# An opening with fifteen early rows of modulation and later bias flips, and the two heads of an attention unit issued apart

## The chip, the core and the metric

The kernel runs on one core of a Trainium2 chip. The metric is the device time of one execution in microseconds (us); a core has a TensorE (PE), a VectorE (DVE), a ScalarE (ACT), a GpSimd (POOL), a SyncE (SP) that here only issues DMAs, and 16 DMA engines. Each engine works through its own list of instructions in order; between engines there are only semaphores.

## The reference

One sequence of 256 tokens, 1024 features, float32, goes through two layers of one model and one of another. What matters here is the start of the first layer:

```python
shift, scale, gate = split(silu(c) @ ada_w[0, 0] + ada_b[0, 0], 3)      # c: 1024, ada_w: 1024 x 3072
h = rms_norm(x, norm_w[0, 0]) * (1 + scale) + shift
x = x + gate * hybrid_attention_mixer(h, ...)      # h @ w_in, gated linear attention, and
                                                   # sliding-window attention, 8 heads on 2 kv heads,
                                                   # scores + rel_bias[t5_bucket(distance)], then @ w_out
```

The mixer's product `h @ w_in` has 2,320 columns. The bias of the windowed attention depends only on the distance of query and key: a table of 32 buckets by 8 heads is spread over distances. Two MLPs, a pooling mixer, a second attention (8 heads, its own bias of position), retention and a gated feed-forward part follow.

## The kernel before

**Weight blocks.** Every large product runs over weight blocks of 1024 x 256 (1 MB). SP loads block n into `raw[n % 4]`; ACT copies it into a rounded high part (`split_hi`, L1897), DVE subtracts to get the low part (`split_lo`, L1215), and PE makes three products per tile: high by high, high by low, low by high (`product`, L595 to L597; with tokens as rows, L677 to L679). A block is 48 products of 256 columns. Activations are split too: `h_hi` by ACT, `h_lo` by DVE. PE needs `lo_done` of a block before it starts it.

**Banks.** PE writes the blocks to the four G banks of PSUM and all small results to four A banks. Each A bank has a fixed order of uses, written out with `take`: PE waits with `bank_empty` until the use before was read, readers wait with `bank_full` and release with `bank_read`.

**Modulation.** `silu(c) @ ada_w` is made on DVE: `ada_w` comes as 24 rows of blocks, 128 x 1024 each (512 KB), and `ada_sum` multiplies one by a value of `c_silu` for each partition and adds it to an accumulator (L1234; the first of a part is L1229). Rows 0 to 7 are the scale, 8 to 15 the shift, 16 to 23 the gate. POOL issues the loads (L522) into three buffers `ada_raw` in turn, each after the row before in that buffer was used; eight rows, named in `ADA_EARLY`, have places of their own in `raw[1]` to `raw[3]`, `GE` and `GG` and are asked for at once (L530). `ada_next(count)` in DVE's list sets when the sums are made. The sum over partitions is left: `turn_sums` has PE transpose the accumulator (L705, 8 transposes) into two A banks, and `part` on DVE reduces each bank along its row (L1260) and adds the bias. ACT has another form of that reduction, `rows_along` (L1912), used in later layers only.

**The opening.** SP issues constants, `c`, x, thirteen small loads of vectors, `rel_bias`, the gate's small weights, then (after DVE has copied the table out of its bank) the table's write to DRAM, weight block 0, and, after ten modulation rows are used, the read of the shifted bias rows, 1 MB, each partition one element further (`hankel`, which is `MIX`). PE transposes x (L781), the vectors, makes the table, the mean squares (L803), the scale's transposes, four `flip` products of 512 columns that turn the bias rows over (L810), the shift's transposes, eight clock-keeping products (`keep_clock`, L622), and block 0 with a wait before each pair of feature tiles. The normalised pairs are made by DVE (x times gain times root, L1377), rounded by ACT with the shift added (`high_norm`, L1934) and subtracted by DVE (L1360). ACT copies the flips to `BIAS` (L2006) before it. Behind block 0 come the gate's rank product, a transpose, block 1 and the logits.

**Attention.** A unit is a pair of heads and a block of 128 queries: `scores` (L737), bias, maximum, exponent and scale on DVE and ACT, `turned` (transposes, L749) and `weighted` (L759). The two heads of a unit lie in the two halves of the partitions and write one bank. Inside `scores`, PE waits for the first head's product before it issues the second's:

```python
for e in range(2):
    ...
    last = pe.matmul(dst[:, e, 0:keys], Q4[half, hp, b * P:b * P + P], K4[half, kt, 0:keys], start=True, stop=True)
    if e == 0:
        chain(last)
```

In the first layer the eight units are written out by hand between the halves of blocks 2 to 8 (`first_half`, `second_half`); in the later attention, `attention(1, v)` on PE puts scores of unit v, transposes of v - 1 and the output of v - 2 behind one another between blocks. The gate's transposes stand between the halves of blocks 2 and 3.

## Time and profile before

| what | us |
|---|---|
| median of 3 runs (947.22 to 949.34) | 948.78 |
| the profiled execution | 948.3 |
| its span, first to last instruction | 946.6 |
| PE busy, share | 893.9, 94% |
| DVE / ACT / POOL busy | 684.8 / 463.6 / 84.5 |
| mean granted TensorE clock, of full | 0.991 |

Times in rows are us from the start of the span, of one execution. "Idle before" says what ended the wait of an engine in front of an instruction. Durations of matmuls overlap; the distance between starts is what counts.

### The profile page before, as it was taken

How to read it: one execution, taken by the hardware profiler on the slowest of the kernel's cores; microseconds unless marked ns; L12 is line 12 of the kernel's file. 1: busy time of each engine (PE TensorE's matmuls, PEld its weight loads, DVE VectorE, ACT ScalarE, POOL GpSimd, SP SyncE). 2: the span in 40 equal slices, each digit the busy share in tenths (PEclk: the TensorE clock that was granted, in tenths of full speed). 3: DMA queues.
4: the chain of work that ended last, by engine and by line, in shares of the span. 5: the costliest groups of instructions: out<-in, count | busy, mean ns of one | idle time of the engine just before them, and what ended most of it. 6: DMA issues, size and time to landing. Idle time of an engine off the chain costs nothing.

```text
span 946.6 us, 17770 instructions
## 1 busy us (share of the span) xinstructions
PE 893.9 (94%) x7084; PEld 855.4 (90%) x7084; DVE 684.8 (72%) x857; ACT 463.6 (49%) x623; POOL 84.5 (9%) x140
## 2 busy tenths in 40 slices
PE   2699989899999999899999999999999999999996
PEld 2488879899999999799999999888989999999996
DVE  4889888788897887766665556765587777775665
ACT  2348464466663335466653334544565444444445
POOL 2210148211110110000000000000000000000000
PEclk9899999999999999999999999999999999999998
DMA  9895754499996886277655553844435655655531
GB/s 340 301 358 185 243 200 158 139 318 320 327 359 232 311 305 218 74 238 222 222 200 178 181 188 119 254 135 134 134 109 166 201 188 182 199 166 177 162 119 44
DMA packets 156603, 196.64 MB, mean 208 GB/s; under 512 B 5341, under 2 KB 143116, under 8 KB 156556
## 3 DMA queue, kind: packets, MB, share of 16 engines
q1 hardware_dynamic: 142732, 145.64, 48.1%
q0 software_dynamic: 13824, 50.34, 14.2%
q8 instruction: 33, 0.54, 0.2%
q14 instruction: 14, 0.11, 0.0%
HBM read 194.90 MB, written 1.06 MB: 207 GB/s over the span
## 4 chain that ended last, share of the span: by engine, by line
PE 77%; DVE 10%; ACT 5%; DMA 4%; issue 3%; SPq 1%; POOL 0%; ACTq 0%; DVEq 0%; POOLq 0%
PE G L595 14%; PE G L597 14%; PE G L596 14%; PE A L595 7%; PE A L597 7%; PE A L596 7%; DVE w_lo L1215 3%; ACT w_hi L1897 2%; PE G L677 2%; PE G L678 2%; PE G L679 2%; PE A L737 2%; DMA ada_raw<-in_ada_w_dram 1%; DMA sinks<-in_attn_sinks_dram 1%; DVE ada_acc L1234 1%
## 5 line engine op out<-in xcount | busy, mean ns | idle before, releaser
L1215 DVE TENSOR_TENSOR w_lo<-raw,w_hi 128x2048 fp32r<-128x2048 f32 x135 | 307.0, 2274 | 159.3 <-ACT w_hi L1897 158.8
L1897 ACT ACTIVATE w_hi<-raw 128x2048 fp32r<-128x2048 f32 x135 | 256.5, 1900 | 246.5 <-PE G L597 130.0
L595 PE MATMUL G<-h_hi,w_hi 128*128 128x256 f32 x864 | 248.8, 288 | 9.3 <-DVE h_lo L1360 6.8
L596 PE MATMUL G<-h_lo,w_hi 128*128 128x256 f32 x864 | 245.1, 284 | 0.0
L597 PE MATMUL G<-h_hi,w_lo 128*128 128x256 f32 x864 | 245.0, 284 | 0.0
L595 PEld LDWEIGHTS G<-h_hi,w_hi 128*128 128x128 f32 x864 | 166.2, 192 | 15.6 <-DVE h_lo L1360 6.5
L596 PEld LDWEIGHTS G<-h_lo,w_hi 128*128 128x128 f32 x864 | 166.4, 193 | 0.2 <-issue 0.2
L597 PEld LDWEIGHTS G<-h_hi,w_lo 128*128 128x128 f32 x864 | 166.3, 193 | 0.0
L595 PE MATMUL A<-u_hi,w_hi 128*128 128x256 f32 x512 | 145.3, 284 | 1.6 <-DVE X L1338 1.2
L596 PE MATMUL A<-u_lo,w_hi 128*128 128x256 f32 x512 | 144.1, 282 | 0.0
L597 PE MATMUL A<-u_hi,w_lo 128*128 128x256 f32 x512 | 144.1, 281 | 0.0
L595 PE MATMUL G<-e_hi,w_hi 128*128 128x256 f32 x368 | 104.1, 283 | 0.0
L596 PE MATMUL G<-e_lo,w_hi 128*128 128x256 f32 x368 | 104.1, 283 | 0.0
L597 PE MATMUL G<-e_hi,w_lo 128*128 128x256 f32 x368 | 104.1, 283 | 0.0
L595 PEld LDWEIGHTS A<-u_hi,w_hi 128*128 128x128 f32 x512 | 96.4, 188 | 3.5 <-DVE X L1338 1.8
L596 PEld LDWEIGHTS A<-u_lo,w_hi 128*128 128x128 f32 x512 | 96.4, 188 | 0.0
L597 PEld LDWEIGHTS A<-u_hi,w_lo 128*128 128x128 f32 x512 | 96.4, 188 | 0.0
L1234 DVE SCALAR_TENSOR_TENSOR ada_acc<-ada_raw,c_silu,ada_acc 128x1024 f32<-128x1024 f32 x52 | 66.1, 1281 | 9.5 <-DMA ada_raw<-in_ada_w_dram 8.5
L595 PEld LDWEIGHTS G<-e_hi,w_hi 128*128 128x128 f32 x368 | 70.7, 192 | 0.0
L596 PEld LDWEIGHTS G<-e_lo,w_hi 128*128 128x128 f32 x368 | 70.7, 192 | 0.0
L597 PEld LDWEIGHTS G<-e_hi,w_lo 128*128 128x128 f32 x368 | 70.7, 192 | 0.0
L595 PE MATMUL A<-f_hi,w_hi 128*128 128x256 f32 x176 | 50.0, 284 | 1.6 <-DVE HN L1332 1.6
(349 smaller groups left out, 1389.7 us busy)
## 6 DMA issues: line engine op xcount, KB each, us to landing
raw<-in_mlp_w_dram SPq DMA_DIRECT2D x64, 1024.0 KB, 5.5
ada_raw<-in_ada_w_dram POOLq DMA_DIRECT2D x88, 512.0 KB, 5.3
raw<-in_w_in_dram SPq DMA_DIRECT2D x14, 1024.0 KB, 5.0
raw<-in_w_up_dram SPq DMA_DIRECT2D x11, 1024.0 KB, 5.3
raw<-in_w_gate_dram SPq DMA_DIRECT2D x11, 1024.0 KB, 5.4
raw<-in_attn_w_in_dram SPq DMA_DIRECT2D x9, 1024.0 KB, 10.3
raw<-in_w_down_dram SPq DMA_DIRECT2D x8, 1024.0 KB, 5.2
raw<-in_attn_w_out_dram SPq DMA_DIRECT2D x4, 1024.0 KB, 5.2
```

Of the source, the lines that this page charges most:

```text
L595: pe.matmul(dst, wh, ah, start=start, stop=False)
L596: pe.matmul(dst, wh, al, start=False, stop=False)
L597: return pe.matmul(dst, wl, ah, start=False, stop=stop)
L677: pe.matmul(dst, h_hi[:, t, toks], w_hi[n % 2][:, t, cols], start=t == 0, stop=False)
L678: pe.matmul(dst, h_hi[:, t, toks], w_lo[n % 2][:, t, cols], start=False, stop=False)
L679: last = pe.matmul(dst, h_lo[:, t, toks], w_hi[n % 2][:, t, cols], start=False, stop=t == KT - 1)
L737: last = pe.matmul(dst[:, e, 0:keys], Q4[half, hp, b * P:b * P + P], K4[half, kt, 0:keys], start=True, stop=True)
L1215: dve.tensor_tensor(w_lo[n % 2][:, 0:k, :], raw[n % RAW][:, 0:k, :], w_hi[n % 2][:, 0:k, :].bitcast(F32), ALU.subtract).then_inc(lo_done, 1)
L1234: dve.scalar_tensor_tensor(out=acc, in0=src, scalar=c_silu[:, bass.ds(i * 2 + k, 1)], in1=acc, op0=ALU.mult, op1=ALU.add).then_inc(ada_use ...
L1897: act.activation(w_hi[n % 2][:, 0:k, :], raw[n % RAW][:, 0:k, :], ACT.Copy).then_inc(hi_done, 1)
```

## The change

- Fifteen modulation rows (3 to 15, 19 and 20) have places of their own: five in `raw[1]` to `raw[3]`, the rest in buffers that attention uses later. POOL asks for all but row 15 at once; for that one it waits for the table's write, since it shares its place.
- SP's order becomes constants, c, `rel_bias`, small loads, the table's write, x, block 0, the gate's small loads, the bias rows; then it waits until row 14 has landed, and loads blocks 1 to 3 once the rows in their places are used.
- POOL makes x times root (four products of 128 x 512) in place of DVE, and waits for weight block 1 before it asks for row 16. ACT applies gain and shift in one operation and does it twice, for `h_hi` and for a float32 copy `HN1`, from which DVE subtracts in one operation a pair. The scale's sums and half of the shift's are reduced by ACT (`rows_along`).
- PE: the table first, x behind the vectors; eight clock-keeping products more behind the scale's transposes; the four flips behind block 0; ACT copies them behind the keys of block 0.
- The gate's transposes go behind the last unit of the first attention, ahead of block 9; ACT reduces them ahead of the split of block 10.
- `scores` takes a head. The wait goes from the first head's issue to the second's, which is placed in the next block behind two of its eight steps (six products), or behind other small products.

```diff
-ADA_EARLY = (3, 4, 5, 6, 7, 8, 19, 20)
+ADA_EARLY = (*range(3, 16), 19, 20)
...
-                 for n in range(6)] + [b[:, :, :].rearrange("p t s -> p (t s)") for b in (GE, GG)]
+                 for n in range(5)]
+        early += [b[:, :, :].rearrange("p t s -> p (t s)") for b in (Q4, K4, V4, GV)] + [
+            PT[:, :, :, :].rearrange("p a b s -> p (a b s)"),
+            wide[:, 4:6, :].rearrange("p a b -> p (a b)"), wide[:, 6:8, :].rearrange("p a b -> p (a b)"),
+            SS[:, :, :, :].rearrange("p a b s -> p (a b s)")]
+        early += [b[:, :, :].rearrange("p t s -> p (t s)") for b in (GE, GG)]
...
@@ SP
-                sp.dma_start(x_rows, x[0].rearrange("(k p) d -> p k d", p=P)).then_inc(x_in, 16)
+                sp.dma_start(rb[:, :], rel_bias).then_inc(rb_in, 16)
...
+                bank_was_read(sp, "table")
+                sp.dma_start(scratch.ap(), t8[:, :]).then_inc(table_out, 16)
+                sp.dma_start(x_rows, x[0].rearrange("(k p) d -> p k d", p=P)).then_inc(x_in, 16)
+                load(N_ATTN, w_in[:, :, ATTN_COLS[0]:ATTN_COLS[0] + COLS])
...
-                sp.wait_ge(ada_used, 10)
                 sp.dma_start(hankel[:, :, :],
...
+                sp.wait_ge(early_full[ADA_EARLY.index(2 * DT - 2)], 16)
...
-                        sp.wait_ge(ada_used, (14, 16, 16)[j - 1])
+                        sp.wait_ge(ada_used, (5, 7, 8)[j - 1])
@@ POOL
+                if f == 2 * DT - 1:
+                    pool.wait_ge(table_out, 16)
+                if f == 2 * DT:
+                    pool.wait_ge(rstd_ready, 1)
+                    for p in range(4):
+                        pool.tensor_tensor(HN0[:, 2 * p:2 * p + 2, :], X[:, 2 * p:2 * p + 2, :],
+                                           spread(rstd[:, :], 2), ALU.mult).then_inc(norm_ready, 1)
+                    pool.wait_ge(raw_full[1], 16)
@@ PE, a block's tile
                 for a, (kb, ka) in enumerate(kts):
+                    if inside and a == 2:
+                        scores(*inside)
@@ PE, scores(r, v, e)
+                if e == 0:
+                    bank_empty(pe, f"scores{r}{v}")
+                else:
+                    pe.wait_ge(score_first, ATT_UNITS * r + v + 1)
...
+                if e == 0:
+                    last.then_inc(score_first, 1)
+                else:
+                    bank_done(f"scores{r}{v}", last)
@@ PE, attention(r, v)
-                    scores(r, v)
+                    scores(r, v, 0)
                 if 1 <= v <= ATT_UNITS:
                     turned(r, v - 1)
+                if v < ATT_UNITS:
+                    scores(r, v, 1)
@@ PE, order
             turn_sums(0, "scale", DT)
-            pe.wait_ge(table_in, 16)
-            for q in range(4):
-                dst = bank_empty(pe, f"flip{q}")
...
-            turn_sums(0, "shift", 2 * DT)
+            keep_clock(0, 8)
+            turn_sums(0, "shift", 2 * DT)
             keep_clock(0, 8)
             feature_block(0, 0, split="n0")
+            pe.wait_ge(table_in, 16)
+            for q in range(4):
+                dst = bank_empty(pe, f"flip{q}")
...
-            scores(0, 0)
-            first_half(2)
-            scores(0, 1)
-            second_half(2)
-            turn_sums(0, "gate", ADA_B)
+            scores(0, 0, 0)
+            first_half(2, inside=(0, 0, 1))
+            scores(0, 1, 0)
+            second_half(2, inside=(0, 1, 1))
...
             weighted(0, 7)
+            turn_sums(0, "gate", ADA_B)
@@ DVE
-            chain(part(0, "scale"))
-            factor(0)
-            split_lo(0)
-            ada_next(4)
-            part(0, "shift").then_inc(mod_ready, 1)
...
+            ada_next(9)
+            for half in "ab":
+                bank_was_read(dve, f"scale0{half}")
+            chain(with_bias(DT, DT, DT))
+            chain(factor(0))
+            ssq[0] = 4
+            ada_next(2)
+            split_lo(0)
...
-            norm("n0", 0, GAIN[:, 0, :], MOD[:, 0, 0:DT])
+            for p in range(4):
+                low_pair("n0", p, HN1[:, 2 * p:2 * p + 2, :])
...
-            chain(part(0, "gate"))
@@ ACT
+            root(0)
+            for half in range(2):
+                src = bank_full(act, f"scale0{'ab'[half]}")
+                bank_read(f"scale0{'ab'[half]}", rows_along(src, DT + 4 * half))
...
+            src = bank_full(act, "shift0a")
+            bank_read("shift0a", rows_along(src, 0))
             act.wait_ge(mod_ready, 1)
-            high_norm("n0", MOD[:, 0, 0:DT])
+            for p in range(4):
...
+                for dst in (h_hi, HN1):
+                    for t in (2 * p, 2 * p + 1):
+                        ins = act.activation(dst[:, t, :], HN0[:, t, :], ACT.Identity,
+                                             scale=GAIN[:, 0, t:t + 1], bias=MOD[:, 0, t:t + 1])
+                ins.then_inc(hhi_ready, 1)
...
+            for half in range(2):
+                src = bank_full(act, f"gate0{'ab'[half]}")
+                bank_read(f"gate0{'ab'[half]}", rows_along(src, 2 * DT + 4 * half))
             split_hi(10)
```

`with_bias` adds the bias to sums that `rows_along` left; it exists before.

## Rows read from the trace of the kernel before

**Rows 1.** The page's first part: busy time of each engine over the span.
```profile
PE 893.9 (94%) x7084; PEld 855.4 (90%) x7084; DVE 684.8 (72%) x857; ACT 463.6 (49%) x623; POOL 84.5 (9%) x140
```

**Rows 2.** PE timeline to 55 us: start, us, line, op, tiles, count, [idle before].
```profile
12.13 1.97 PE L781 MATMUL A<-C,wide 128*128 128x128 f32 x8 [7.61 <-DMA wide<-in_x_dram]
...
35.97 5.32 PE L810 MATMUL A<-MIX,C 128*128 128x512 f32 x8 [7.47 <-DMA MIX<-bias_rows]
41.12 1.04 PE L705 MATMUL A<-C,ada_acc 128*128 128x128 f32 x8
41.99 3.62 PE L622 MATMUL G<-C,ones 128*128 128x256 f32 x16
...
50.88 0.38 PE L595 MATMUL G<-h_hi,w_hi 128*128 128x256 f32 x1 [0.15 <-DVE h_lo L1360]
...
54.57 0.28 PE L595 MATMUL A<-h_hi,g_hi 128*16 128x256 f32 x1
```

**Rows 3.** DVE timeline: the sixteenth modulation row, block 15.
```profile
39.59 1.28 DVE L1234 SCALAR_TENSOR_TENSOR ada_acc<-ada_raw,c_silu,ada_acc 128x1024 f32<-128x1024 f32 x1 [1.15 <-DMA ada_raw<-in_ada_w_dram]
```

**Rows 4.** Stretches: length, busy PE, PEld, DVE, ACT, POOL, clock, DMA share, GB/s.
```profile
0.00:10.00 10.00, 0.24 (x1) 0.18 (x1) 3.06 (x10) 2.74 (x3) 5.07 (x13) 1.00 0.76 281
10.00:20.00 10.00, 2.68 (x11) 2.07 (x11) 5.88 (x6) 2.06 (x4) 1.59 (x3) 1.00 1.04 391
...
35.00:36.00 1.00, 0.03 (x1) 0.04 (x1) 0.57 (x2) 0.00 (x0) 0.36 (x1) 0.50 1.04 421
```

**Rows 5.** ACT timeline: bias copy, normalised pair, key copy, two steps of line 1912.
```profile
41.32 0.60 ACT L2006 ACTIVATE BIAS<-A 128x512 f32<-128x512 f32 x1 [0.26 <-PE A L810]
...
48.94 0.91 ACT L1934 ACTIVATE h_hi<-HN,MOD 128x256 fp32r<-128x256 f32 x2 [0.80 <-DVE HN L1377]
...
54.77 0.39 ACT L2013 ACTIVATE wide<-G 128x256 f32<-128x256 f32 x1 [3.12 <-PE G L597]
...
376.38 0.26 ACT L1912 ACTIVATE A<-A 128x128 f32<-128x128 f32 x1 [1.48 <-PE A L705]
...
376.64 0.27 ACT L1912 ACTIVATE A<-A 128x128 f32<-128x128 f32 x1
```

**Rows 6.** POOL and DVE timelines while both read on-chip memory.
```profile
136.81 0.46 POOL L563 TENSOR_TENSOR C<-band,C 128x128 f32<-128x128 f32 x1
...
156.95 2.29 DVE L1215 TENSOR_TENSOR w_lo<-raw,w_hi 128x2048 fp32r<-128x2048 f32 x1
...
157.11 2.21 POOL L561 TENSOR_TENSOR C<-C 128x16 f32<-128x16 f32 x1
```

**Rows 7.** The gate's transposes, and the way into block 9: PE, ACT and DVE timelines.
```profile
72.88 1.04 PE L705 MATMUL A<-C,ada_acc 128*128 128x128 f32 x8
...
78.68 0.41 PE L749 MATMUL A<-C,PR 128*128 128x128 f32 x2 [0.75 <-DVE part_sums L1260]
...
139.06 0.67 PE L759 MATMUL A<-PT,V 128*64 128x128 f32 x8 [1.83 <-ACT MIX L1974]
...
141.55 0.52 PE L595 MATMUL G<-h_hi,w_hi 128*128 128x256 f32 x1 [0.80 <-DVE h_lo L1357]
...
142.67 1.90 ACT L1897 ACTIVATE w_hi<-raw 128x2048 fp32r<-128x2048 f32 x1
...
144.60 2.29 DVE L1215 TENSOR_TENSOR w_lo<-raw,w_hi 128x2048 fp32r<-128x2048 f32 x1 [1.11 <-ACT w_hi L1897]
...
148.48 0.28 PE L597 MATMUL G<-h_hi,w_lo 128*128 128x256 f32 x1
```

**Rows 8.** Line 737: its idle time in total and times; PE timeline around one unit.
```profile
PE A L737: 5.9, 16
...
83.44 0.28 PE L597 MATMUL G<-h_hi,w_lo 128*128 128x256 f32 x1
83.64 1.45 PE L737 MATMUL A<-K,Q 64*128 64x256 f32 x4
85.02 0.39 PE L595 MATMUL G<-h_hi,w_hi 128*128 128x256 f32 x1
```

133 lines of the change are left out of this document (73 added, 60 removed).

## The prediction

> **What bounds the kernel now.** I read the page's busy part first: PE works 94% of the span [rows 1], so from some point on every microsecond that leaves PE's own line leaves the total, and the question is where PE still waits. The PE timeline answers it: after 50 us PE waits only some 8 us in all, and nearly all the idle time lies in the opening, where it waits for x, then 7.47 us for the flipped bias rows, and then for the first normalised pairs [rows 2]. The bias rows are not what sets the end of the opening: the shift's transposes need the sixteenth modulation row, whose sum ends at 39.59 + 1.28 = 40.87 us after a wait of 1.15 us for its DMA [rows 3]. The stretches say why it is late: from 10 to 20 us the DMA engines are full at 391 GB/s [rows 4], and still block 15 was asked for late, because three buffers alone took most of the rows. From 40.87 us a fixed tail runs: transposes, sums, pairs, the first block; PE leaves block 0 at 54.57 us, 13.7 us later [rows 2].
>
> **The opening, DMA.** The change asks for fifteen of the sixteen rows at once and moves x behind the small loads and the bias table's writing, with weight block 0 and the bias rows (1 MB each) behind x. Before block 15 can land, 16 x 0.52 MB of modulation, 3 x 1.05 MB, and some 0.65 MB of small loads must: 12.2 MB. By 20 us 2.8 + 3.9 = 6.7 MB moved [rows 4]; the other 5.5 MB at 391 GB/s take 14.1 us, so it lands at 34.1 us and its sum ends at 35.4 us. If the bias rows come behind it, it is 2.7 us sooner; if the mixed queues run at 350 GB/s, 1.6 us later. On DVE the sixteen sums take some 20 us and do not bind by themselves.
>
> **The opening, POOL.** The four products of x and the root move from DVE to POOL, 128x512 each. The nearest row is a product of 128x128 in 0.46 us [rows 6]; so one takes between 0.5 (if the start is all of it) and 1.8 us (four times), and I take 1.4, nearer to the upper end since the width is four times. x is now issued at some 8.5 us instead of 1.7 and lands at about 16.5 instead of 12.1 [rows 2], so the root is there at 23 to 24 us: the products fall among DVE's last eight sums. Rows 6 hold the point: POOL's 16-column product, begun at 157.11 behind a two-input DVE operation at 156.95, ends with it, 2.21 us later; both read on-chip memory and do not overlap. Four products can then push the sums by up to 5.6 us; DVE's slack against the DMA (1.28 for a sum, 1.34 to 2.3 for a row that shares the engines) takes up more than half. I take +2.0, so 37.4 us; ends 0 and 5.6 [rows 4, 6]. The Trainium skill has a rule that speaks against this part (SBUF — State Buffer, section "SBUF: two separate sides"): VectorE and GpSimd share one pair of ports as an exclusive lock, held for a whole instruction, where the one has two operands in on-chip memory and the other reads it; whichever comes second waits. By that rule, the trace agrees [rows 6]; taken in full against a busy DVE it would put the sum 3.6 us higher, and without it the sum is 2.0 lower.
>
> **The tail.** By 35 us PE had stood idle and its clock was at half, the 1.2 GHz level [rows 4]; before, the flips brought it back ahead of the shift's transposes. Now these meet it: 0.5 us for the first four instead of half of 1.04 [rows 2] becomes 1.0. ACT sums rows in four steps of 0.26 + 0.19 us, overlapping, some 1.1 us [rows 5], in place of two DVE reductions. The weight split on DVE (2.29 us, as rows 6) lies beside this, and mod_ready comes at +2.7 us. A pair costs ACT four operations in place of two: 2 x 0.91 less the overlap, 1.7 us [rows 5]; four pairs and the last 128x512 difference give +10.1 us, against 50.88 - 40.87 = 10.0 before [rows 2]. The eight clock-keeping products (3.62 us, up to 7 at half clock) fit before that. Block 0 ends at 37.4 + 13.8 = 51.2 us. The pairs on POOL are done by then and hidden, unless the root is 10 us later than I think.
>
> **The flips.** Their four products lay in a stretch where PE waited; now they stand between blocks on PE's line with no cover. They move as many columns as the clock-keeping ones, which at full clock took 3.62 us [rows 2] (5.32 was partly at half clock). The next user of the bank waits for the last bias copy: 0.2 + 0.60 [rows 5]. ACT's key copies (four of 0.39) run beside. PE reaches the gate rank product at 51.2 + 3.6 + 0.8 = 55.6 us instead of 54.57: **+1.0**. What the opening gains, the flips take. Weight block 1, issued when row 14 is in, has 15 us, and stays hidden; SP's other loads queue behind it and are not needed before 60 us.
>
> **The gate.** Eight transposes leave PE's line at 72.88 (-1.0) and with them the wait of 0.75 for their bank [rows 7]. They return behind the last attention unit, where PE waits 0.80 before the second pair: +0.2 there. But ACT now sums eight rows (8 x 0.29 = 2.3 us [rows 5]) ahead of the split of weight block 10. Its low part, 144.60 to 146.9, shifts to about 149.2, and PE wants it at 148.6 [rows 7]: a new wait of 0.6, which swallows the 0.2. Sum -1.0 - 0.75 + 0.6: **-1.15**. Bounds: -2.9, if the gap that was filled also keeps the clock up, and +0.6, if block 9 itself runs sooner and the split counts in full.
>
> **The heads.** PE stood 5.9 us in 16 units between the two heads, 0.37 each [rows 8]. In seven units the second head goes into the next block, which adds one more change of operand kind: entering costs 83.64 - 83.44 = 0.20 [rows 8] where the block's own pitch is 0.12 (30 products from 50.88 to 54.57 us [rows 2]), so 0.08; leaving I set at as much, and 0.2 is left of each: -1.4. In eight units other small products stand between, with no added change: 0.3 each, -2.4. One (second attention, first unit) has nothing between and keeps its wait. DVE gets seven of the scores some 0.7 us later, and has the slack. **-3.8**; bounds 0 and -5.9. Nothing else waits on PE in these stretches, so this reaches the end.
>
> **Sum.** The profiled run took 948.3 us (span 946.6, 1.7 around it), 0.5 under the median of 948.78. 948.3 + 1.0 - 1.15 - 3.8 = 944.4 us. A measurement of this kernel can tell about 0.2%, 1.9 us, from no change.
>
> **The rivals.** *No quarrel for the memory port:* the products fall into DVE's gaps while it waits for rows. For: DVE idles before rows in the opening [rows 3]. Against: rows 6. Then 2.0 less, 942.4. *The opening comes late:* x behind fifteen rows lands at 20 us or more, or port and small transfers add their upper ends, and the sixteenth sum ends at 41 us as before, so that the flips are paid in full: 948.0. For: x takes half the engines at best, and the 64-byte pieces of the gate's rank load stand in its queue. *The heads bring nothing*, because the idle time shown is the array's draining and comes back at each change: 944.4 + 3.8 = 948.2. *Slower:* every isolated head pays the whole overhead of a unit. A 256-key unit takes 85.02 - 83.64 = 1.38 us [rows 8] for four steps of the clock-keeping product's size (3.62 / 16 = 0.23 each [rows 2]), so some 0.47 are overhead; paid twice in 15 units that is +7.1 in place of -3.8: 955.3. It decides from a loss of 0.14 us a unit on, as opening and gate nearly cancel. Against it: 0.37 of the 0.47 is shown as a wait for the first head, which six products in between must cover.
>
> **How the numbers follow.** Forecast 0.42 (own range 942.9 to 946.3); no quarrel 0.22; opening late 0.15; heads nothing 0.12; heads dearer 0.09. The first two are faster by over 0.2%, with a quarter of the late case: 0.68. Within 0.2%: 0.22. Slower: 0.10. The range takes the first four with their bounds and leaves out the dear heads and the clock gain in full: 940.5 to 949.5.
>
> **What would show it.** The sixteenth sum ends at 36 to 39 us, with DVE sums stretched or spaced beside POOL's four products; flips of 3.6 us behind block 0 and a wait of under 1 us after; no wait inside line 737's units but one; no wait at 78 us and a new one of some 0.6 us before block 10; PE busy unchanged otherwise. A sixteenth sum after 40 us, or a clock at half through block 0, or pitches around the split heads over 0.3 us would prove me wrong.

## The result and the profile after

| | before | changed |
|---|---|---|
| median, us (18 runs each) | 949.36 (947.22 to 952.92) | 954.81 (950.26 to 958.0) |
| profiled execution, us / span | 948.3 / 946.6 | 953.7 / 952.0 |
| mean granted clock of it | 0.991 | 0.989 |

Ratio 1.0047, 95% interval 1.0034 to 1.006: the change makes the kernel half a per cent slower. The forecast was 944.4, in a range of 940.5 to 949.5. The two profiled spans differ by 5.4 us, as the medians do, so this pair of traces can be read line against line. The start of the same instruction on PE, changed minus before:

| PE reaches | before | changed | shift |
|---|---|---|---|
| the shift's transposes | 41.12 | 37.04 | -4.1 |
| the gate's rank product | 54.57 | 56.44 | +1.9 |
| the transposes of the keys' end | 91.88 | 93.75 | +1.9 |
| the second norm's mean squares | 168.38 | 171.16 | +2.8 |
| the gate's transposes of the first MLP | 283.18 | 287.47 | +4.3 |
| the mean squares behind the first MLP | 371.69 | 377.78 | +6.1 |
| the first products behind the second attention | 675.60 | 681.00 | +5.4 |
| its last product | 938.02 | 943.43 | +5.4 |

The busy times, as rows 1:

```profile
PE 898.3 (94%) x7100; PEld 860.7 (90%) x7100; DVE 680.8 (72%) x841; ACT 473.4 (50%) x671; POOL 92.2 (10%) x144
```

PE is busy 4.4 us longer and the span is 5.4 longer, but 3.6 of the 4.4 are the eight added clock-keeping products, which stand in a wait (26.93 to 30.55 us). So the sums of busy time do not say where the 5.4 went; the starts do. The opening lost 1.9 where 1.0 was forecast. Gate and heads, forecast at -5.0, show no gain in the starts up to the second mean squares. And two things of which the prediction said nothing cost time: DVE's new order of sums, 1.6 us ahead of the keys' end, and the stretch around the first down block, 3.3 us.

**The opening.** DVE timeline of the changed kernel (as rows 3 and 6: start, us, line, op, tiles, count, [idle before]):

```profile
27.62 1.99 DVE L1269 SCALAR_TENSOR_TENSOR ada_acc<-PT,c_silu,ada_acc 128x1024 f32<-128x1024 f32 x1 [0.35 <-DMA PT<-in_ada_w_dram]
29.72 2.10 DVE L1269 SCALAR_TENSOR_TENSOR ada_acc<-wide,c_silu,ada_acc 128x1024 f32<-128x1024 f32 x1
31.74 1.22 DVE L1303 TENSOR_TENSOR MOD<-mod_sums,V 128x8 f32<-128x8 f32 x1
...
35.61 1.28 DVE L1269 SCALAR_TENSOR_TENSOR ada_acc<-SS,c_silu,ada_acc 128x1024 f32<-128x1024 f32 x1
```
The POOL timeline of the same stretch, the four products of x and root:

```profile
27.27 6.90 POOL L545 TENSOR_TENSOR wide<-X,rstd 128x512 f32<-128x512 f32 x4 [12.20 <-ACT rstd L1956]
```

The sums of 1.28 us take 1.99 and 2.10 beside POOL's products, and the two 8-column operations, lines 1303 and 1308, 1.22 and 1.19: some 3.6 us of stretching. The four POOL products take 1.7 us each in the mean, and they are stretched as well: two take 1.26 us and the two that begin beside a sum 2.24. The line's own view says it (shortest, median and longest in ns):

```profile
L545 POOL TENSOR_TENSOR wide<-X,rstd x4: 1262/1750/2242, 27.3 to 32.9; 128x512 f32<-128x512 f32 x4
```

Even so the sixteenth sum ends at 35.61 + 1.28 = 36.9 us, 4.0 sooner than before [rows 3]. PE from there (as rows 2):

```profile
19.25 3.51 PE L815 MATMUL A<-C,wide 128*128 128x128 f32 x16 [4.61 <-DMA wide<-in_x_dram]
...
37.04 1.94 PE L731 MATMUL A<-C,ada_acc 128*128 128x128 f32 x8 [6.49 <-DVE ada_acc L1269]
38.77 5.69 PE L645 MATMUL G<-C,ones 128*128 128x256 f32 x16
...
48.36 0.39 PE L616 MATMUL G<-h_hi,w_hi 128*128 128x256 f32 x1 [0.99 <-DVE h_lo L1392]
...
52.06 3.60 PE L848 MATMUL A<-MIX,C 128*128 128x512 f32 x8
56.44 0.28 PE L616 MATMUL A<-h_hi,g_hi 128*16 128x256 f32 x1 [0.78 <-ACT BIAS L2079]
```

The tail from the sixteenth sum to the end of block 0 takes 52.06 - 36.9 = 15.2 us instead of 13.7. Its pairs are paced by ACT: the sixteen operations start at 39.61 and the next thing at 47.49, so the four of a pair cost 1.97. ACT timeline, the first two:

```profile
39.61 1.09 ACT L2066 ACTIVATE h_hi<-wide,MOD,GAIN 128x256 fp32r<-128x256 f32 x2 [0.23 <-DVE MOD L1506]
```
DVE waits for each pair; its timeline at the last one:

```profile
47.62 0.69 DVE L1392 TENSOR_TENSOR h_lo<-wide,h_hi 128x512 fp32r<-128x512 f32 x1 [1.27 <-ACT wide L2066]
```

The flips then take 3.60 and the wait for the bank 0.78, to the tenth what was forecast. What the clock did in these stretches (length, busy PE, granted clock, DMA share, GB/s):

```profile
30.00:35.00 5.00, 0.55 (x3) 0.77 1.12 334
37.00:39.00 2.00, 1.96 (x9) 0.50 1.11 350
...
41.00:43.00 2.00, 2.00 (x6) 0.51 1.11 357
43.00:45.00 2.00, 2.00 (x13) 1.00 1.04 395
```

PE stands idle from about 31 to 37 us, and its clock is at the lower level, 1.2 GHz, until 43 us; before, it was back by 39.

**Gate and sums.** The wait of 0.75 for the bank [rows 7] is gone, but the transposes of the keys' end now wait, and so does block 10. PE timeline at the two places:

```profile
93.75 0.66 PE L894 MATMUL A<-C,wide 128*128 128x128 f32 x4 [1.43 <-DVE wide L1548]
...
151.12 0.39 PE L616 MATMUL G<-h_hi,w_hi 128*128 128x256 f32 x1 [1.49 <-DVE w_lo L1250]
```
DVE timeline ahead of the first:

```profile
84.65 2.66 DVE L1269 SCALAR_TENSOR_TENSOR ada_acc<-ada_raw,c_silu,ada_acc 128x1024 f32<-128x1024 f32 x2
87.23 0.75 DVE L1264 TENSOR_SCALAR ada_acc<-ada_raw,c_silu 128x1024 f32<-128x1024 f32 x1
...
93.01 0.69 DVE L1548 TENSOR_TENSOR wide<-wide 128x512 f32<-128x512 f32 x1
```
ACT timeline ahead of the second:

```profile
144.57 0.26 ACT L1962 ACTIVATE A<-A 128x128 f32<-128x128 f32 x1
...
146.84 1.90 ACT L1947 ACTIVATE w_hi<-raw 128x2048 fp32r<-128x2048 f32 x1
```

At 84.65 DVE makes three modulation sums in a row (3.2 us) ahead of the split of weight block 5 and of the products that the keys' end needs, which end 1.4 us late; before, one stood at this place, and DVE idles 5.3 us further ahead, from 63.0 to 68.3, where the changed counts could have put them. Before block 10, ACT's eight reductions (144.57 to 146.84) push the split by the 2.3 us that were forecast. PE waits 1.49 where 0.6 was forecast, because it comes to block 10 sooner than the prediction took: counted from the keys' end, block 9 ends 0.65 us earlier than before, although eight transposes now stand ahead of it.

**The heads.** A unit of 128 keys, its first head, then a second head with six products between, and the next unit (PE timeline, as rows 8):

```profile
66.35 0.48 PE L768 MATMUL A<-K,Q 64*128 64x128 f32 x2
...
67.47 0.28 PE L618 MATMUL G<-h_hi,w_lo 128*128 128x256 f32 x1
67.68 0.49 PE L768 MATMUL A<-K,Q 64*128 64x128 f32 x2
68.09 0.39 PE L616 MATMUL G<-h_hi,w_hi 128*128 128x256 f32 x1
...
70.44 0.70 PE L768 MATMUL A<-K,Q 64*128 64x256 f32 x2
```
The wait inside a unit is gone, but it was far smaller than rows 8 made it, as the groups of the second attention show (line, engine, op, tiles, count | busy us, mean ns | idle before); of the kernel before:

```profile
L737 PE MATMUL A<-K,Q 64*128 64x128 f32 (+1 forms) x32 | 9.5, 375 | 0.5
```
and of the changed kernel:

```profile
L768 PE MATMUL A<-K,Q 64*128 64x128 f32 (+1 forms) x32 | 9.5, 375 | 0.1
```

PE stood idle 0.5 us in the eight units of the second attention, 0.06 in each, and not 0.37. The 5.9 us of rows 8 are idle time of the weight load (PEld), whose work overlaps PE's. The view of line 737 in the kernel before says so under "who waited for it":

```profile
  PEld A L737: 5.9, 16
```

In starts, the second head of a unit came 0.12 us later than the instructions inside a head follow one another (0.33 instead of 0.21 with 128 keys, 0.43 instead of 0.32 with 256). That is all that setting the heads apart could save. What it costs: from unit 0's start to unit 1's it is 70.44 - 66.35 = 4.09 us, and before it was 4.02 (64.50 to 68.52). A head alone stands 0.21 behind the last product, where the block's pitch is 0.12, and the first block product behind a head takes 0.22 to its next instead of 0.12. Together that is 0.19 for 0.12 saved.

**Before the first down block.** DVE waits for the rows of the next modulation (DVE timeline):

```profile
285.44 1.28 DVE L1269 SCALAR_TENSOR_TENSOR late_acc<-ada_raw,c_silu,late_acc 128x1024 f32<-128x1024 f32 x1 [1.58 <-DMA ada_raw<-in_ada_w_dram]
```
PE waits to transpose for DVE's reduction behind it (PE timeline):

```profile
287.47 1.29 PE L742 MATMUL G<-C,ada_acc 128*128 128x128 f32 x8 [2.48 <-DVE part_sums L1651]
```
and then the clock is at half (stretches, columns as above):

```profile
289.00:291.00 2.00, 2.00 (x11) 0.50 0.91 347
291.00:293.00 2.00, 2.00 (x15) 0.72 0.64 205
```

Before, this wait was 0.95 us and the clock stayed full. By the starts, the stretch at half clock costs 1.5 us (the shift grows from 4.3 to 5.8).

### The profile page after: what moved, and what is told of

It reads as the page before. It is cut to its first block, busy times and chain, and to the rows that moved or that the text cites. A ratio compares the mean times of both kernels' runs of the same rounds, so it can differ in the third digit from the quotient of the medians.

```text
span 952.0 us, 17830 instructions
## 1 busy us (share of the span) xinstructions
PE 898.3 (94%) x7100; PEld 860.7 (90%) x7100; DVE 680.8 (72%) x841; ACT 473.4 (50%) x671; POOL 92.2 (10%) x144
## 3 DMA queue, kind: packets, MB, share of 16 engines
HBM read 194.90 MB, written 1.06 MB: 206 GB/s over the span
## 4 chain that ended last, share of the span: by engine, by line
PE 75%; DVE 10%; ACT 6%; DMA 4%; issue 3%; POOL 1%; DVEq 0%; ACTq 0%; POOLq 0%
PE G L616 14%; PE G L618 13%; PE G L617 13%; PE A L616 6%; PE A L618 6%; PE A L617 6%; DVE w_lo L1250 3%; ACT w_hi L1947 3%; DMA ada_raw<-in_ada_w_dram 2%; DMA PT<-in_ada_w_dram 2%; PE G L703 2%; PE G L704 2%; PE G L705 2%; PE A L768 2%; DVE ada_acc L1269 1%
## 5 line engine op out<-in xcount | busy, mean ns | idle before, releaser
L1269 DVE SCALAR_TENSOR_TENSOR ada_acc<-ada_raw,c_silu,ada_acc 128x1024 f32<-128x1024 f32 x45 | 57.3, 1285 | 5.1 <-DMA ada_raw<-in_ada_w_dram 4.1
L565 POOL DMA_DIRECT2D ada_raw<-in_ada_w_dram x53 | 28.0, 529 | 251.7 <-DVE late_acc L1269 167.9
```

The lines of the kernel that those rows point to most:

```text
L565: pool.dma_start(ada_raw[ADA_SLOT[f]][:, :], ada[m][:, bass.ds(i, 1), part * D:(part + 1) * D].rearrange("p a n -> p (a n)")).then_inc(ada ...
L1269: dve.scalar_tensor_tensor(out=acc, in0=src, scalar=c_silu[:, bass.ds(i * 2 + k, 1)], in1=acc, op0=ALU.mult, op1=ALU.add).then_inc(ada_use ...
```

## The experiments

All are timed in five rounds beside runs of the kernel before. "Opening" below is the start of the gate's rank product (before 54.57, changed 56.44).

| run | median, us | ratio to before [95%] | opening | keys' end, less opening |
|---|---|---|---|---|
| before | | 1 | 54.57 | 37.31 |
| changed | 954.81 | 1.0047 [1.0034, 1.006] | 56.44 | 37.31 |
| heads as before | 955.14 | 1.0042 [1.0021, 1.0062] | 59.02 | 37.14 |
| gate and sums as before | 952.8 | 1.0038 [1.0021, 1.0055] | 57.86 | 36.62 |
| flips ahead of the shift | 954.79 | 1.0054 [1.0039, 1.007] | 56.08 | 37.33 |
| sums in the old order | 951.96 | 1.0018 [1.0002, 1.0033] | 56.36 | 35.73 |
| before, heads only | 949.99 | 1.0007 [0.9992, 1.0023] | 55.73 | 36.63 |
| before, gate only | 949.6 | 1.0003 [0.999, 1.0015] | 55.23 | 35.51 |
| opening only | 954.07 | 1.004 [1.0018, 1.0062] | 59.61 | 36.37 |
| clock kept | 952.22 | 1.0017 [0.9997, 1.0038] | 56.40 | 35.72 |
| products on DVE | 952.09 | 0.9998 [0.9981, 1.0014] | 56.57 | 35.73 |
| pairs shared | 949.49 | 0.9982 [0.9963, 1.0001] | 54.34 | 35.74 |
| flips inside | 944.86 | 0.9925 [0.99, 0.995] | 49.30 | 35.74 |
| best | 943.36 | 0.9909 [0.9885, 0.9933] | 50.03 | 35.52 |
| flips only | 948.21 | 0.9976 [0.996, 0.9992] | 53.08 | 35.74 |
| order as changed | 945.99 | 0.9954 [0.9939, 0.997] | 49.91 | 37.34 |
| best, gate back | 944.72 | 0.9935 [0.9918, 0.9952] | 50.05 | 36.36 |

From "sums in the old order" on, every run built on the changed kernel has the old order unless it says otherwise. The medians of the kernel before in the four sets of runs were 949.64, 950.0, 951.56 and 950.68, so ratios are compared, not medians, across sets. Each experiment has 12 runs, but six of flips inside, best, and best with the gate back, and ten of heads as before. One of those ten took 2571.3 us, for no reason that the record shows; it is left out of the ratio, and the median is the same without it.

### Undoing one part of the change

**Heads as before** puts both heads of a unit in a row again with the wait between them:

```diff
-                if e == 0:
-                    bank_empty(pe, f"scores{r}{v}")
-                else:
-                    pe.wait_ge(score_first, ATT_UNITS * r + v + 1)
+                for e in range(2):
+                    ...
+                    if e == 0:
+                        chain(last)
```

> The changed kernel with the two heads of each unit issued together again, the first layer's and the later attention's, with the wait between them; opening, flips and gate stay. Theory A (an isolated head pays its own way out of about 0.2 us, so that splitting saves next to nothing): the two profiles differ by 0.3 to 0.5 us in the first attention in favour of the joined heads and by 0.7 us in the later one in favour of the split ones; total within 1 us of the changed kernel. Rival (the split heads cost, as feared in the prediction): 4 to 7 us faster than the changed kernel, about the time of the kernel before.

**Gate and sums as before** undoes the move of the gate's transposes, their banks and reductions, and the order of DVE's sums:

```diff
-            turn_sums(0, "gate", ADA_B)          # behind weighted(0, 7)
+            turn_sums(0, "gate", ADA_B)          # behind second_half(2)
-            ada_next(2) ... ada_next(1) ... ada_next(3)
+            ada_next(5) ... ada_next(1)
```

> The changed kernel with the gate's transposes, banks, reduction on DVE and the order of the modulation sums as before; opening and heads stay. Theory A: the stretch from 70 to 80 us takes 1.6 us more again, the 1.4 us wait for the keys' end factor near 92 us and the 1.5 us wait for the low part of block 10 go: the first attention ends 1 us sooner or the same. Rival 1 (moving the gate is what the loss comes from): 2.5 us faster than the changed kernel. Rival 2 (the move pays, as predicted): 1 us slower.

**Flips ahead of the shift** puts them where the kernel before has them:

```diff
             turn_sums(0, "scale", DT)
-            keep_clock(0, 8)
+            pe.wait_ge(table_in, 16)
+            for q in range(4):
+                ...
             turn_sums(0, "shift", 2 * DT)
```

> The changed kernel with the four flips put back ahead of the shift's transposes, where PE waits from 30.5 to 37 us, in place of the eight clock-keeping products... and with their copies on ACT ahead of the shift's sums. Theory A (the flips behind block 0 cost their 3.6 us and the 0.8 us wait in full, and the bias rows have landed by about 32 us): block 1 starts 4 to 4.5 us sooner, PE's clock is full at the shift's transposes, total 4 to 5 us faster than the changed kernel, about the kernel before or 1 us faster. Rival (the bias rows land late, at 36 us or more, since SP could only issue them from 17 to 28 us): the shift's transposes wait for them, and it gains 1 us or less.

**Sums in the old order** changes only three counts on DVE:

```diff
             split_lo(2)
-            ada_next(2)
+            ada_next(5)
...
             scaled(0, 0)
-            ada_next(1)
...
             scaled(0, 2)
-            ada_next(3)
+            ada_next(1)
```

> The changed kernel with the modulation sums 21 to 23 made where DVE idles for 5.3 us ahead of the first scores, as in the kernel before, instead of three of them in a row behind the third unit. Theory A: the wait of 1.4 us for the keys' end factor near 92 us goes, 1.2 us faster at the end of the first attention, total 1 to 1.5 us faster. Rival (the loads of these rows have not landed by 63 to 67 us, or the later modulation ring of layer 0 falls into the same pattern anyway): no difference within 1 us.

The heads, the gate and the flips put back change nothing that the timing can tell: their intervals overlap the changed kernel's. The old order's interval ends just below it (1.0033 against 1.0034). The traces say more. With the old order the wait before the keys' end is gone: the last column falls from 37.31 to 35.73, 1.6 us, and the ratio from 1.0047 to 1.0018. With the flips ahead of the shift, PE waits for the bias rows and the shift's transposes stand behind them (PE timeline, flips first):

```profile
35.02 5.13 PE L842 MATMUL A<-MIX,C 128*128 128x512 f32 x8 [7.27 <-DMA MIX<-bias_rows]
39.99 1.04 PE L731 MATMUL A<-C,ada_acc 128*128 128x128 f32 x8
```

The rows land at 35 us, 1.4 before the sixteenth sum ends in this trace, so this order costs the shift's transposes 3 us and saves the flips' 3.6 and the wait of 0.8 behind the block; the opening gains 0.4 and the total nothing. In this trace the clock also fell to half late in block 0 (0.65 granted from 51 to 53 us, 0.50 from 53 to 55), which hides about 1 us of what the order is worth.

What I did not expect: the opening's own end, with the same code in it, is at 56.4 in some runs and 57.9 and 59.0 in others. The stretches of the run with the heads as before show why:

```profile
45.00:47.00 2.00, 1.00 (x9) 1.00 1.05 396
...
49.00:51.00 2.00, 2.00 (x11) 0.50 1.02 389
```

PE is partly idle from 43 to 49 us, one pair every 2 us with 1.0 us of work in it, and after that its clock is granted at half, over the long end of block 0. It is so in four of the traces with ACT's long pairs (heads as before, gate as before, flips ahead, opening only) and not in three (changed, sums in the old order, products on DVE). Why it falls in one execution and not in another is open. The kernel before has 1.1 to 1.3 us of work in 2 there and kept its clock in its trace; heads only, with the same opening, had 0.95 and 1.06 in two such stretches and kept it too.

### One part alone

**Before, heads only** and **before, gate only** apply one part to the kernel before; **opening only** takes the changed kernel without the other two parts and with the old order of sums.

```diff
# heads only
-            scores(0, 0)
-            first_half(2)
+            scores(0, 0, 0)
+            first_half(2, inside=(0, 0, 1))
# gate only
             weighted(0, 7)
+            turn_sums(0, "gate", ADA_B)
```

> The kernel before with nothing changed but the two heads of all 16 attention units set apart; opening and gate as they were. By the prediction's sum (idle of 0.37 a unit goes, 0.08 to 0.17 comes): 3.8 us faster, 945 us, ratio 0.996. By what the changed kernel's trace shows: the head costs its drain wherever it stands, so each unit of the first attention costs 0.05 to 0.14 more and each of the second 0.12 less: between -0.5 and +0.4 us, ratio 1.000; block products beside units b=0 4.09 instead of 4.02 us, b=1 4.45 instead of 4.36, second attention's second head 0.63 + 0.63 instead of 1.38. Rival: the heads set apart delay DVE and cost over 1 us elsewhere: ratio over 1.001.

> The kernel before with the gate sums' transposes moved behind the last attention unit and their rows summed by ACT, the sums on DVE in the old order. By the prediction's sum: -1.15 us, ratio 0.999 (1.75 off PE's line at 72 to 79 us, and a new wait of 0.6 before block 10). By what the changed kernel's trace shows: the same gain, no wait at the shift of the keys' end (kend), since the sums on DVE keep their order, but a new wait of 1.5 us before block 10 or its split: -0.25 us. Rival: the time moved is paid twice, at block 10 and at the first down block's gate transposes: over +1 us, ratio 1.001 or more.

> The changed kernel with heads and gate as before and DVE's sums behind block 0 in the old order: only the opening is changed. Theory: the opening is the loss. PE reaches the gate rank product 1.9 us late when the clock holds through block 0, and up to 4.5 us late when it falls to half in it, so median +2 to +3.5 us, ratio 1.002 to 1.0037. By the prediction's sum: +1.0, ratio 1.001. Rival: the loss is interplay of opening and gate (late loads and sums), so that the opening alone costs under 1 us, ratio under 1.001.

The heads alone bring 1.0007, the gate alone 1.0003, the opening alone 1.004 (with a late opening in its trace, 59.61): the opening is the loss. In the traces the gate alone gains 1.8 us up to the keys' end and gives 0.8 back by 168 us, -1.0 in all; the forecast was -1.15. Its 1.8 are 1.0 of transposes and the wait of 0.75 for a bank [rows 7]. That wait is also gone in the trace of the heads alone, which gains 0.7 between the rank product and the keys' end, and in that of the opening alone (36.37 against 37.31), so it counts once. It need not be the work of any of the three. Ahead of it DVE makes three modulation sums; in the trace of the kernel before it waits 2.05 us for their DMA, in that of the heads alone not at all, with the same instructions on DVE there but an opening 1.2 us later. The first of the three, before and with the heads alone (DVE timelines):

```profile
64.17 1.28 DVE L1234 SCALAR_TENSOR_TENSOR ada_acc<-ada_raw,c_silu,ada_acc 128x1024 f32<-128x1024 f32 x1 [1.24 <-DMA ada_raw<-in_ada_w_dram]
...
64.19 4.06 DVE L1249 SCALAR_TENSOR_TENSOR ada_acc<-ada_raw,c_silu,ada_acc 128x1024 f32<-128x1024 f32 x3
```

In the second attention the heads alone gain 0.7 us (from 582.75 to 675.60 it was 92.85 us before, now 92.14), 0.09 a unit. The gains cannot be told in the total, where the openings of single runs scatter by more.

**Clock kept** adds products whose results nobody uses:

```diff
             turn_sums(0, "scale", DT)
-            keep_clock(0, 8)
+            keep_clock(0, 18)
...
                     if split and a % 2 == 0:
+                        if split == "n0" and a:
+                            keep_clock(1, 2)
                         pe.wait_ge(h_ready, 4 * SPLIT[split] + a // 2 + 1)
```

> The changed kernel with DVE's sums in the old order (as in the run of that name), ten more clock-keeping products behind the scale's transposes and two between each two of block 0's pairs; none of their results is used. If the half clock in the opening is a cost, the shift's transposes take 1.0 instead of 1.9 us, the clock stays at the 2.4 GHz level from 30 to 55 us, PE reaches the gate rank product 0.5 to 1 us sooner than 56.4 us in every run, and the spread of the single runs (some 6 us) shrinks: median 1 to 2 us under the run with the sums in the old order, ratio 0.999 to 1.001 against the kernel before. If the clock there does not matter (ACT's pairs and DVE's split set the pace): no change, ratio 1.0018. Rival: the added products stand in front of something that would have been ready: slower than 1.0018.

Stretches of this run (columns as above):

```profile
37.00:39.00 2.00, 1.80 (x13) 1.00 1.10 348
...
49.00:51.00 2.00, 2.00 (x19) 1.00 1.04 395
```

The clock is full throughout, and in all 12 runs the mean granted clock was 0.994 to 0.998 (0.985 to 0.992 in the changed kernel's 18). But the rank product comes at 56.40, as in the traces whose clock held, and the ratio is the same (1.0017, old order 1.0018): in the opening the shift's transposes are quicker, and ACT's pairs then set the pace all the same. What it removes, by the clocks of its 12 runs and this one trace, is the bad case of 58 to 60 us. The runs still scatter (949.1 to 954.95); in this profile PE waits 3.0 us before the first down block, so the scatter has a second source there.

### Where the opening's time goes

**Products on DVE** tests the memory port:

```diff
-                    pool.wait_ge(rstd_ready, 1)       # POOL
-                    for p in range(4):
-                        pool.tensor_tensor(HN0[...], X[...], spread(rstd[:, :], 2), ALU.mult).then_inc(norm_ready, 1)
             chain(factor(0))
+            dve.wait_ge(rstd_ready, 1)                # DVE
+            for p in range(4):
+                dve.tensor_tensor(HN0[...], X[...], spread(rstd[:, :], 2), ALU.mult).then_inc(norm_ready, 1)
```

> The changed kernel with DVE's sums in the old order, and the four products of x and root on DVE behind the factor instead of on POOL. If POOL's products hold the port against DVE (lock): the sums beside them take 1.28 us again instead of 1.99 and 2.10, the 8-column products 0.17 instead of 1.2, some 3.6 us in all; DVE pays four products of 0.7 in their place, so the sixteenth sum ends at 36 to 36.5 us instead of 36.9, or later if DVE then waits for rows. If there is no lock (rows late, or a slow stretch of DVE): the sums stay at 2 us and the sixteenth ends 2.8 us later. End to end within 1 us of the run with the sums in the old order either way, ratio 1.001 to 1.003.

DVE timeline of that run:

```profile
31.55 0.16 DVE L1298 TENSOR_TENSOR MOD<-mod_sums,V 128x8 f32<-128x8 f32 x1
31.75 0.17 DVE L1303 SCALAR_TENSOR_TENSOR GAIN<-MOD,V 128x8 f32<-128x8 f32 x1
31.95 2.50 DVE L1495 TENSOR_TENSOR wide<-X,rstd 128x512 f32<-128x512 f32 x4
...
35.74 1.28 DVE L1264 SCALAR_TENSOR_TENSOR ada_acc<-SS,c_silu,ada_acc 128x1024 f32<-128x1024 f32 x1
```

Everything beside POOL's products is at its own length again (1.28; 0.16 and 0.17 for the 8 columns), so the stretching was theirs. By the Trainium skill (SBUF — State Buffer, "SBUF: two separate sides") a GpSimd operation that reads on-chip memory and a VectorE operation with two on-chip inputs take a shared port pair in turn, each for a whole instruction; the trace agrees: 1.28 becomes 1.99 and 2.10, and POOL's own 1.26 becomes 2.24. But the four products cost DVE 2.5 us, and the sixteenth sum ends at 37.0, not sooner. Behind the landing of its row (32.75 us in the changed kernel, 33.52 here) it ends 4.1 us later with the products on POOL and 3.5 with them on DVE. So moving them to POOL bought nothing; the ratios, 1.0018 and 0.9998, have intervals that overlap.

**Pairs shared** gives half of ACT's work on a pair to DVE, which sat idle 1.2 us in each; ten more clock-keeping products stand behind the scale's transposes.

```diff
# ACT
-                for dst in (h_hi, HN1):
-                    for t in (2 * p, 2 * p + 1):
-                        ins = act.activation(dst[:, t, :], HN0[:, t, :], ACT.Identity, ...)
+                for t in (2 * p, 2 * p + 1):
+                    ins = act.activation(h_hi[:, t, :], HN0[:, t, :], ACT.Identity, ...)
# DVE
             for p in range(4):
+                for t in (2 * p, 2 * p + 1):
+                    ins = dve.tensor_scalar(HN1[:, t, :], HN0[:, t, :], GAIN[:, 0, t:t + 1],
+                                            MOD[:, 0, t:t + 1], ALU.mult, ALU.add)
                 low_pair("n0", p, HN1[:, 2 * p:2 * p + 2, :])
```

> The changed kernel with the sums in the old order, ten more clock-keeping products behind the scale's transposes, and each first-block pair shared out: ACT makes the high part alone (two operations), DVE makes the whole value for the subtraction itself (two operations with scale and shift) in place of ACT's third and fourth. If ACT's four operations (1.97 us a pair) make the long tail of the opening: a pair costs 1.4 to 1.6 us, block 0 ends at 49.5 to 50.5 us instead of 52.1, and the end comes 1.5 to 2.5 us sooner than in the changed kernel with the clock kept: ratio 0.999 to 1.000. If DVE's weight split or the flips' copies bind: block 0 sooner, the gate rank product still at 56 us, ratio 1.0015. Rival: what the opening gains, the modulation rows' DMA before the first down block takes back: milestones sooner up to 280 us, the same behind.

**Flips inside** adds to it that the flips stand in block 0's waits; ACT copies them ahead of the keys of block 0 instead of behind:

```diff
                     if split and a % 2 == 0:
+                        if split == "n0" and a:
+                            flip(a // 2)
                         pe.wait_ge(h_ready, 4 * SPLIT[split] + a // 2 + 1)
...
-            keep_clock(0, 8)
+            keep_clock(0, 4)
+            pe.wait_ge(table_in, 16)
+            flip(0)
             feature_block(0, 0, split="n0")
```

> As the run with the pairs shared, and the flips moved from behind block 0 into the waits for its pairs (the first ahead of pair 0, one behind each of pairs 0, 1 and 2), four clock-keeping products instead of eight ahead. If the flips' place on PE's own line is what turns the earlier sixteenth sum into a loss: 3.6 + 0.8 us go from behind block 0, 0.5 to 1.5 comes back as pairs that wait behind a flip; the gate rank product at 50.5 to 52.5 us instead of 56.4 (before: 54.57), the end 2 to 4 us sooner than before: ratio 0.996 to 0.998. Rival: block 1 or 2 then wait for their weights, or the rows before the first down block take it back: ratio 0.999 to 1.000.

PE timeline of the run with the flips inside:

```profile
39.32 1.10 PE L643 MATMUL A<-MIX,C 128*128 128x512 f32 x2 [0.28 <-DVE part_sums L1512]
...
41.71 1.02 PE L643 MATMUL A<-MIX,C 128*128 128x512 f32 x2
42.21 0.64 PE L616 MATMUL G<-h_hi,w_hi 128*128 128x256 f32 x1
...
49.30 0.28 PE L616 MATMUL A<-h_hi,g_hi 128*16 128x256 f32 x1
```
DVE timeline of the same run, the first pair and the start of the second:

```profile
39.29 0.76 DVE L1523 TENSOR_SCALAR wide<-wide,GAIN,MOD 128x256 f32<-128x256 f32 x2
40.08 0.69 DVE L1395 TENSOR_TENSOR h_lo<-wide,h_hi 128x512 fp32r<-128x512 f32 x1
40.69 0.73 DVE L1523 TENSOR_SCALAR wide<-wide,GAIN,MOD 128x256 f32<-128x256 f32 x2
```

A pair is 40.69 - 39.29 = 1.40 us instead of 1.97, the three waits in block 0 are gone, and the flips of 1.02 us each begin where the waits were. Pairs shared moves the rank product by -2.0 (56.36 to 54.34), the flips inside by another -5.0. Part of that is the executions' own: the sixteenth sum ends at 36.82, 37.43 and 36.09 us in the three traces. Counted from it, the rank product comes 2.6 us sooner by the pairs and 3.7 by the flips. The ratio goes from 1.0018 to 0.9982 to 0.9925.

**Best** has the flips inside and the heads of units 0 to 6 in a row again:

```diff
-            scores(0, 0, 0)
-            first_half(2, inside=(0, 0, 1))
+            scores(0, 0, 0)
+            scores(0, 0, 1)
+            first_half(2)
```

> As the run with the flips inside, and the two heads of the first attention's units 0 to 6 in a row again, as before (unit 7 and the second attention keep them apart). If a head alone costs its drain: 0.05 to 0.14 us less in each of seven units than with the heads apart, some 0.7 us in all, ratio 0.0007 lower; below what the timing tells apart, so the profile's block products beside those units decide (4.02 and 4.36 against 4.09 and 4.45 us). By the prediction's sum it would be 1.4 us slower.

Unit 0 to unit 1 is 4.02 us again, against 4.08 with the heads apart, and the stretch from the rank product to the last unit's output is 0.4 us shorter: 0.05 a unit. That is what a head alone costs; the 0.0007 expected in the ratio can't be told (the intervals overlap).

### What was left open after these

> The changed kernel with the sums in the old order and the flips in the waits of block 0's pairs, but ACT's four operations a pair and the clock-keeping products as in the changed kernel. If the flips' place is the main loss of the opening: 3.6 + 0.8 us leave PE's line behind block 0 and at most 0.4 comes back, since a pair's wait (0.6 to 1.0 us) nearly holds a flip of 0.9: the gate rank product at 52 to 53 us instead of 56.4, ratio 0.997 to 0.9985. The flips also keep PE busy, so that its clock should not fall in block 0. If the pairs and the clock matter more: 54 us or later, ratio about 1.000.

> As the run with the flips inside, but with DVE's sums behind block 0 in the changed kernel's order (two behind the split of block 2, three ahead of the split of block 5 and of the keys' end). If the order costs what the changed kernel's trace shows: a wait of 1 to 1.5 us before the keys' end's transposes that the run with the flips inside has not, and some 0.5 us more later on: 1.5 to 2 us slower than it, ratio 0.9945. If the wait was only a child of the late opening: no wait there, ratio 0.9925 as before.

> As the best run, but with the gate's transposes, banks and sums where the kernel before has them. By the prediction's step (1.75 us gained at 72 to 79 us, a new wait before block 10 of 0.6) and by the run with the gate alone (1.8 gained at the keys' end, 0.8 given back by 168 us): 1.0 to 1.2 us slower than the best run, ratio 0.992. Rival: the modulation rows before the first down block take the gain back, so that the ends are the same: ratio 0.991.

**Flips only** is the diff of the flips inside without the shared pairs and with the changed kernel's clock-keeping products. It turns 1.0018 into 0.9976: the place of four flips alone decides between a loss and a gain. Its clock stayed full from 43 us on, with PE busy throughout. **Order as changed** has the changed kernel's three counts on the run with the flips inside; its trace has the wait back at the keys' end (PE timeline):

```profile
87.25 0.66 PE L897 MATMUL A<-C,wide 128*128 128x128 f32 x4 [1.44 <-DVE wide L1558]
```

The ratio is 0.9954 against 0.9925, near the 0.9945 expected, though the intervals overlap. **Best, gate back** is 0.9935 against 0.9909, 2.5 us by the ratios; the intervals overlap. In the two traces the gate at its old place costs 0.84 us up to the keys' end, near the 1.0 of its transposes; the 0.75 for their bank does not come back. And the wait before the first down block is 1.8 us there and 3.2 in the best, and that run's span is the shorter one. That the gate's move is worth its microsecond in the total is not shown.

## Why the prediction was wrong

Forecast and profiled execution are 9.3 us apart (944.4 and 953.7). The step that failed most is the heads' (3.5 us); then come the first down block (3.3) and DVE's order of sums (1.6), which the sum put at nothing, and the tail of the opening (0.9 in the end). Heads at nothing and a late opening lay in the range; the two terms at nothing, 4.9 us, did not, and without them the profiled execution would stand at 948.8, inside it. The rival "heads dearer" named 955.3, close to the measured 954.8, but that is luck: it asks for 7 us lost at the heads, and they lost nothing.

**The sixteenth sum: right in the end, by parts that cancel.** It ends at 36.9 us for 37.4. Its row landed at 32.75 us and not at 34.1: the bias rows came behind it (35.4 us), the case that the prediction priced at -2.7 and did not take. POOL's products then pushed the sums by 2.9 us and not by 2.0. x landed at 19.2 us where 16.5 was forecast, and the root was ready at 27.2 instead of 23 to 24, so the products fell beside the thirteenth and fourteenth sum and the two 8-column operations. One product is 1.26 us unstretched and 2.24 stretched, where I took 1.4.

**The tail: too short by 1.4 us.** The step "A pair costs ACT four operations in place of two: ... 1.7 us" measured 1.97, in each of four pairs, about 1.1 us; the last 0.3 lie between the last pair and PE's products (0.87 us from ACT's last operation to them). The row of 0.91 was of operations with a bias alone; with scale and bias, two take 1.09 by the profile and start 0.49 apart. The steps before were right: the shift's transposes took 1.94 for eight at half clock (1.0 for the first four, as counted), and the first pair began at 39.61, 2.7 behind the sum. So were the flips, 3.60, and the wait, 0.78. Opening +1.9 instead of +1.0.

**What the tail did to the clock: missed.** I had named "a clock at half through block 0" as what would prove me wrong, and gave it no price. Longer pairs mean a PE that works 1.0 us in 2, and in four of seven traces its clock then fell; in the three of them whose opening is otherwise the changed one, the rank product came at 57.86, 59.02 and 59.61 instead of 56.4, 1.4 to 3.2 us later (0.9 of the 3.2 is a later sixteenth sum). In the changed kernel's own trace the clock held through block 0, so this is no part of the 5.4 us above. Its other executions run the same risk: the four shortest spans (948.5 to 951.2) have granted clocks of 0.99 and more, the longest (956.3) 0.985, though the half clock behind the first down block lies in the same mean.

**The gate: near by itself, wrong beside the rest.** Alone it is -1.0 for a forecast of -1.15 (1.8 gained, 0.8 given back), but 0.75 of the gain is the bank's wait, which was gone without it as well. The step "PE wants it at 148.6 [rows 7]: a new wait of 0.6" failed: ACT's reductions push the split as counted, but PE comes 1.0 us sooner, and the wait is 1.49 (1.21 with the gate alone). The bounds had named it: block 9 itself runs sooner. And the prediction read the opening's diff as if DVE's list behind block 0 were the same. The changed counts (2, 1, 3 in place of 5 and 1) were in the diff, and no step priced them: three sums ahead of a split, 1.6 us at the keys' end, the largest omission that a run of its own shows.

**The heads: wrong.** The step "PE stood 5.9 us in 16 units between the two heads, 0.37 each" failed. The 5.9 us are the weight load's idle time, which PE's work covers; PE itself stood 0.06 us in each unit, and by the starts 0.12 could be saved, under 2 us in 16 units. The costs "0.08 to enter, as much to leave" were near what runs show (0.09 and 0.10), so in the first attention they eat the 0.12. The whole step, forecast at -3.8, measures +0.05 in each unit of the first attention and -0.09 in each of the second: about -0.3. The rival that "the heads bring nothing" had the size, at 0.12, though not by the reason that it gave: there was nearly nothing to gain.

**The first down block: not seen.** The wait there grew from 0.95 to 2.5 us and 1.5 more went at half clock. In the seventeen traces this wait is between 0.9 and 3.2 us, and the longer ones (over 2.4) stand with early openings as well as late ones, so it isn't the opening's doing alone. In five of the seven with such a wait the clock fell to half, for some 3 us, in the wait or behind it (not in gate as before, 2.56, nor clock kept, 3.02); of the ten others it fell in one, best with the gate back, 1.76. It is where the modulation rows' DMA arrives last, and what makes one execution later than another I have not settled.

The sum again, by the traces. Opening +1.9. To the keys' end 0: the bank's wait gone -0.95 (opening only, 36.37), heads +0.25 (gate as before, 36.62), gate -0.9 (old order, 35.73), order +1.6 (37.31). To 168 us +0.9: -0.65 up to the end of block 9, +1.65 at the wait before block 10, -0.1 behind it. Then +3.3 at the first down block, 1.5 of wait, 1.5 of clock and 0.3 in small pieces up to 368 us, and -0.7 in the second attention: 5.4. Terms under 0.5 us are of single traces and can as well be an execution's own.

## What to carry to other kernels

Work that stood in a wait is free; moved to let something else come earlier, it is paid in full, so look for the next wait that it fits, here the gaps between the pairs (3.6 us from the sixteenth sum to the rank product, by the flips alone). Before a wait is priced, see whose it is: a weight load that waits under running products costs nothing, and the distance between PE's starts, 0.12 us longer here and not 0.37, is what can be saved. And when buffers let rows come earlier, the order in which the consumer takes them is a second change, to be priced on its own.

## What the runs showed of the hardware

- A head's two instructions on 64 rows between products on 128: 0.21 us from the last product to the first of them, and 0.41 from there to the next product with 128 columns (0.63 with 256), where the block's pitch is 0.12. Apart or in a row makes 0.06 us a unit.
- POOL's product of 128 x 512 with two on-chip operands takes 1.26 us, and 2.24 when it begins beside a sum on DVE; DVE's takes 0.62. DVE's 8-column operation beside it takes 1.2 instead of 0.16.
- An issue on SP can itself take long. In the changed kernel the issue of a small load behind x and weight block 0 took 5.84 us, that of the bias rows 11.27 (SP timeline), where before they took 0.42 and 0.37. It is so in all 13 traces that have this opening (5.5 to 6.4 and 10.4 to 11.5 us); what SP waits for in them is not shown:

```profile
9.89 5.84 SPq L454 DMA_DIRECT2D w_gla<-in_gla_w_gate_dram  x1
...
17.17 11.27 SPq L459 DMA_DIRECT2D MIX<-bias_rows  x1
```

- With 1.0 us of work in 2 between pairs, PE's clock fell to the lower level in four of seven traces and held in three, with the same products in block 0; with the flips between the pairs it held in all of them.
